# Tile halves in the output product, first rows copied by ScalarE, router sums in the retention stage

## What is computed

```python
for layer in range(DEPTH):
    y = _even_mixer(h, ...) if layer % 2 == 0 else _odd_mixer(h, ...)
    h = _layer_norm(DN_ALPHA * h + y, ln_w[layer, 0], ln_b[layer, 0])
    y = _moe(h, router_w, moe_w_gate[layer], moe_w_up[layer], moe_w_down[layer])
    h = _layer_norm(DN_ALPHA * h + y, ln_w[layer, 1], ln_b[layer, 1])

def _moe(h, router_w, w_gate, w_up, w_down):
    probs = softmax(x @ router_w)
    # the best group of four experts, and the top two inside it
    # tokens sorted by expert; hid = silu(x @ w_gate[e]) * (x @ w_up[e]); y = hid @ w_down[e]
```

## Time and profile before

| | before |
|---|---|
| median of 3 runs | 1387.13 us (1386.0 to 1387.42) |
| the profiled execution | 1386.77 us |
| its span in the trace | 1384.9 us |
| TensorE busy | 1335.2 us, 96% |
| VectorE busy | 528.3 us, 38% |
| chain of work that ended last | PE 86%, DVE 9% |
| granted TensorE clock, mean | 0.983 |

### The profile page before, as it was taken

One profiled execution on the slowest core, in us unless ns is written; L12 is line 12 of the kernel. 1 busy time (PEld: TensorE's weight loads), 2 busy tenths in 40 slices (PEclk: granted clock), 3 DMA queues, 4 the chain that ended last, 5 costly groups with the idle time before them and its releaser, 6 DMA issues.

```text
span 1384.9 us, 16143 instructions
## 1 busy us (share of the span) xinstructions
PE 1335.2 (96%) x6723; PEld 604.2 (44%) x6723; DVE 528.3 (38%) x1008; ACT 189.8 (14%) x319; POOL 167.2 (12%) x126
## 2 busy tenths in 40 slices
PE   8999999989999999999999999999898899999996
PEld 4444464533333333344555555555545333333332
DVE  1344762453111111430365666665636221111117
ACT  0025400100000000011111111111111000000000
POOL 0000400041000000200122332222300500000011
PEclk9999989999999999999999999999999999999998
DMA  9920065188999997643321122200094789999943
GB/s 352 370 74 1 31 273 212 53 318 312 410 420 406 422 405 290 247 116 111 90 61 37 25 61 61 61 0 0 4 390 182 294 327 426 402 427 407 426 178 150
DMA packets 83993, 305.84 MB, mean 221 GB/s; under 512 B 6516, under 2 KB 50904, under 8 KB 71512
## 3 DMA queue, kind: packets, MB, share of 16 engines
q1 hardware_dynamic: 61872, 264.65, 49.0%
q10 hardware_dynamic: 17448, 23.46, 4.7%
q0 software_dynamic: 4608, 16.78, 3.2%
HBM read 271.31 MB, written 33.55 MB: 220 GB/s over the span
## 4 chain that ended last, share of the span: by engine, by line
PE 86%; DVE 9%; DMA 1%; issue 1%; ACT 1%; POOL 0%; DVEq 0%; POOLq 0%; SPq 0%
PE ps L596 24%; PE ps L759 14%; PE ps L631 12%; PE ps L475 8%; PE ps L553 7%; PE ps L746 4%; PE ps L781 4%; PE ps L811 2%; PE ps L581 2%; PE ps L545 1%; DVE S L1590 1%; PE ps L534 1%; PE ps L619 1%; PE ps L799 1%; PE ps L521 1%
## 5 line engine op out<-in xcount | busy, mean ns | idle before, releaser
L596 PE MATMUL ps<-W,S 128*32 128x512 f32 (+1 forms) x2048 | 338.5, 600 | 2.2 <-DVE S L1513 2.2
L759 PE MATMUL ps<-hT,W 128*128 128x512 f32 x512 | 232.6, 593 | 0.7 <-ACT W L890 0.7
L596 PE MATMUL ps<-S 128*64 128x512 f32 (+1 forms) x512 | 224.8, 597 | 0.4 <-DVE S L1513 0.4
L631 PE MATMUL ps<-W,hT 128*32 128x512 f32 (+1 forms) x1024 | 171.5, 601 | 1.0 <-DVE hT L1527 1.0
L596 PEld LDWEIGHTS ps<-W,S 128*32 128x32 f32 (+1 forms) x2048 | 97.6, 114 | 150.1 <-issue 145.8
L759 PEld LDWEIGHTS ps<-hT,W 128*128 128x128 f32 x512 | 92.9, 191 | 90.3 <-issue 88.4
L631 PE MATMUL ps<-S,hT 128*32 128x512 f32 (+1 forms) x256 | 113.0, 594 | 1.0 <-DVE hT L1527 1.0
L890 ACT ACTIVATE hT<-ps 128x512 f32<-128x512 f32 x74 | 42.3, 598 | 376.7 <-PE ps L631 287.0
L596 PEld LDWEIGHTS ps<-S 128*64 128x64 f32 (+1 forms) x512 | 62.1, 124 | 71.8 <-issue 70.5
L1721 POOL TENSOR_TENSOR W<-S,sq 128x256 f32<-128x256 f32 x64 | 73.5, 1149 | 160.9 <-PE ps L781 117.3
L475 PE MATMUL ps<-W,hT 128*128 128x512 f32 x192 | 85.5, 604 | 2.1 <-DMA W<-w_in_even 2.1
(11 more groups left out here) (246 smaller groups left out, 1346.7 us busy)
## 6 DMA issues: line engine op xcount, KB each, us to landing
W<-moe_w_gate SPq DMA_DIRECT2D x24, 2048.0 KB, 12.3
W<-moe_w_up SPq DMA_DIRECT2D x24, 2048.0 KB, 13.1
W<-moe_w_down SPq DMA_DIRECT2D x24, 2048.0 KB, 11.4
S<-moe_w_gate SPq DMA_DIRECT2D x8, 2048.0 KB, 13.5
S<-moe_w_up SPq DMA_DIRECT2D x8, 2048.0 KB, 13.8
S<-moe_w_down SPq DMA_DIRECT2D x8, 2048.0 KB, 16.7
W<-w_in_odd SPq DMA_DIRECT2D x32, 512.0 KB, 6.3
slot_rows<-S ACTq DMA_DIRECT2D x4, 2816.0 KB, 20.0
```

The lines of the kernel that those rows point to most:

```text
L596: last = pe.matmul(ps[a:a + n, bank, :], xgT[:, c, a:a + n], w[L][slot_of(e)][:, c, :], start=(c == 0), stop=(c == ND - 1))
L631: last = pe.matmul(ps[a:a + n, 2 + half, :], hidT[:, c, a:a + n], wd[L][slot_of(e)][:, c, half * 512:(half + 1) * 512], start=(c == 0), st ...
L759: last = pe.matmul(ps[:, f % 2, :], ring[slot][:, f, c, :], hT[:, c, :], start=(c == 0), stop=(c == ND - 1))
```

## The change

It has four parts.

1. **Router sums later.** `router_sums(0)` and `router_spread(0)` leave the input projections on PE. They now stand in the retention loop (after the scores of head 1, and after the scores of head 3) in bank 7. VectorE's `router_terms(0)` follows the `prob` of head 1 and `spread_terms(0)` the `prob` of head 2, ahead of the `head_norm` of head 0.
2. **Tile 3 in halves.** Half 0 of tile 3 is transposed inside output product k = 7, in place of the second half of tile 2's logits; these follow behind the product (`last_logits`). VectorE adds and measures half 0 of tile 3 before half 1 is there, and ScalarE copies each half as it comes.
3. **Centre of tile 3 later.** `centre` of tile 3 moves from ahead of `route` to just ahead of tile 3's `shift`, between the third and the fourth selection. PE's products with the selections run tile by tile, both halves of each.
4. **ScalarE copies the first rows.** Half 1 of the first rows, and both transposed halves, are copied by ScalarE in place of VectorE. PE waits for `slots_done` before `up(0)`, since `up(0)` writes the bank that the slots are computed from.

The core of the diff (the same edits as at `logits(0, ...)` stand for layer 1, and the `halves` arguments are passed through in `turn_h`, `turn_copies`, `scale_output`, `statistics` and `add`):

```diff
-            project(4)
-            router_sums(0, 3)
-            project(5)
-            router_spread(0, 3)
-            for n in (6, 7):
+            for n in range(4, 8):
                 project(n)
...
             for hd in range(HR):
                 if hd + 1 < HR:
                     scores(hd + 1)
+                if hd == 0:
+                    router_sums(0, 7)
+                elif hd == 2:
+                    router_spread(0, 7)
                 pe.wait_ge(prob_done, (hd + 1) * NT)
...
+            def last_logits(L):
+
+                logits(L, 2, range(4, ND))
+                turn_h(2 * L + 1, NT - 1, (1,))
+                logits(L, NT - 1, range(4))
+                logits(L, NT - 1, range(4, ND))
...
-                for half in range(2):
-                    for t in range(NT):
-                        pe.wait_ge(sel_done, L * NT + t + 1)
+                for t in range(NT):
+                    pe.wait_ge(sel_done, L * NT + t + 1)
+                    for half in range(2):
                         last = pe.matmul(ps[:, 2 + half, :], first_sel[:, t, :], h[:, t, half * 512:(half + 1) * 512],
                                          start=(t == 0), stop=(t == NT - 1))
-                    last.then_inc(side_ps, 1)
+                        if t == NT - 1:
+                            last.then_inc(side_ps, 1)
...
                     gate(u)
+                    if u == 0:
+                        pe.wait_ge(slots_done, L + 1)
                     up(u)
...
                     out_project(k, mixT, w_out0, range(4), True, False)
                     logits(0, 1)
-                    logits(0, 2)
+                    turn_h(1, NT - 1, (0,))
+                    logits(0, 2, range(4))
                     out_project(k, mixT, w_out0, range(4, ND), False, True).then_inc(op_ps, 1)
...
-            turn_h(1, NT - 1)
-            logits(0, NT - 1)
+            last_logits(0)
             spin(1, 6)
...
                 copy(first_rows[:, 0:512], ps[:, 2, :]).then_inc(side_copied, 1)
+                act.wait_ge(side_ps, 3 * L + 2)
+                copy(first_rows[:, 512:1024], ps[:, 3, :]).then_inc(side_copied, 1)
+                for half in range(2):
+                    act.wait_ge(xgT_ps[L], half + 1)
+                    copy(xgT[:, half * 4:half * 4 + 4, :],
+                         ps[:, 4 + half, :].rearrange("p (c n) -> p c n", c=4)).then_inc(xgT_done[L], 1)
...
+                if hd == 1:
+                    router_terms(0)
+                elif hd == 2:
+                    spread_terms(0)
                 if hd >= 2:
                     head_norm(hd - 2)
...
-                add(3)
-                statistics(n, 3)
+                add(3, (0,))
+                v.bn_stats(col("st", 0, 6), h[:, 3, 0:512])
+                add(3, (1,))
+                statistics(n, 3, (1,))
                 for t in range(3):
                     scaled_logits(L, t)
-                centre(n, 3)
+                dve.wait_ge(std_done, n * NT + 4)
+                done(v.reciprocal(col("rst1", 3, 1), col("std", 3, 1)))
                 done(scaled_logits(L, 3))
...
                     if t == NT - 1:
+                        centre(2 * L, t)
                         shift(t)
...
-                dve.wait_ge(side_ps, 3 * L + 2)
-                v.tensor_copy(first_rows[:, 512:1024], ps[:, 3, :]).then_inc(side_copied, 1)
-                copy_rows(0)
                 hidden(0, first=True)
```

More of the change, by code:

```diff
@@ L429, in _, with turn_h @@
         def _(pe):
-            def turn_h(n, t):
+            def turn_h(n, t, halves=(0, 1)):
                 if n == 0:
@@ L434, in turn_h @@
                 elif n % 2:
-                    pe.wait_ge((op_used, op_added)[n // 2], 2 * t + 2)
+                    pe.wait_ge((op_used, op_added)[n // 2], 2 * t + halves[-1] + 1)
                 else:
                     pe.wait_ge(ln_done, (n - 1) * NT + t + 1)
-                for half in range(2):
+                for half in halves:
                     for c in range(4):
@@ L555, in out_project, with logits @@
                 return last
-            def logits(L, t):
-                pe.wait_ge(hT_done, (2 * L + 1) * 2 * NT + 2 * t + 2)
+            def logits(L, t, chunks=range(ND)):
+                pe.wait_ge(hT_done, (2 * L + 1) * 2 * NT + 2 * t + (1 if chunks[-1] < ND // 2 else 2))
                 pe.wait_ge(prmC, L + 2)
-                for c in range(ND):
+                for c in chunks:
                     last = pe.matmul(ps[:, 0 if t < NT - 1 else 2, t * NE:(t + 1) * NE], hT[:, c, t * P:(t + 1) * P], rw[:, c, :],
                                      start=(c == 0), stop=(c == ND - 1))
-                last.then_inc(logits_ps, 1)
+                if chunks[-1] == ND - 1:
+                    last.then_inc(logits_ps, 1)
+            def last_logits(L):
[3 more added lines that the diff above has]
+                logits(L, NT - 1, range(4, ND))
             def router(L):
@@ L871, in _ @@
                     logits(1, 1)
-                    logits(1, 2)
+                    turn_h(3, NT - 1, (0,))
+                    logits(1, 2, range(4))
                     out_project(k, OG, w_out1, range(4, HG), False, True).then_inc(op_ps, 1)
@@ L879, in _ @@
                     logits(1, 0)
-            turn_h(3, NT - 1)
-            logits(1, NT - 1)
+            last_logits(1)
             spin(1, 6)
@@ L890, in copy, with turn_copies @@
                 return nc.scalar.activation(o, i, ACT.Copy)
-            def turn_copies(n, t):
-                for k in (2 * t, 2 * t + 1):
+            def turn_copies(n, t, halves=(0, 1)):
+                for k in (2 * t + half for half in halves):
                     act.wait_ge(hT_ps, n * 2 * NT + k + 1)
@@ L1114, in _, with scale_output @@
             act.wait_ge(rms_done, 1)
-            def scale_output(t):
-                for k in (2 * t, 2 * t + 1):
+            def scale_output(t, halves=(0, 1)):
+                for k in (2 * t + half for half in halves):
                     act.wait_ge(op_ps, 2 * NT + k + 1)
@@ L1132, in _ @@
             turn_copies(3, 2)
-            scale_output(3)
-            turn_copies(3, 3)
+            for half in range(2):
+                scale_output(3, (half,))
+                turn_copies(3, 3, (half,))
             norm_std(2, 3)
@@ L1194, in _ @@
             v.tensor_tensor(col("lbe", 8, 8), lb1, col("lbm"), ALU.subtract).then_inc(prm_sub, 1)
-            spread_terms(0)
             for n in range(LRU_BLOCKS):
@@ L1303, in tile_of, with statistics @@
                 return halves, ps[:, 2 * t:2 * t + 2, :] if n % 2 else halves
-            def statistics(n, t):
+            def statistics(n, t, halves=(0, 1)):
                 _, src = tile_of(n, t)
-                for half in range(2):
+                for half in halves:
                     last = v.bn_stats(col("st", 6 * half, 6), src[:, half, :])
@@ L1372, in add_mixer, with add @@
             def add_mixer(L):
-                def add(t):
-                    for half in range(2):
+                def add(t, halves=(0, 1)):
+                    for half in halves:
                         k = 2 * t + half
@@ L1384, in add @@
                                                    ).then_inc(op_added, 1)
-                    dve.wait_ge((op_used, op_added)[L], 2 * t + 2)
+                    dve.wait_ge((op_used, op_added)[L], 2 * t + halves[-1] + 1)
                 return add
```

15 lines of the change are left out of this document (7 added, 8 removed).

## The result

The change takes **1379.66 us** (median of 5 runs, 1378.46 to 1380.36) against 1387.13 before: a ratio of 0.9948, 95% interval 0.9934 to 0.9963, or 7.2 us less. I had forecast 1382.9 and a range down to 1380.3.

A forecast was written before the change was run, and what follows sets the result against it. TensorE, busy 96% of the span, was taken as the bound. Terms -4.7 and -5.5 (turns), +2.8 (retention), +3.0 (clock) and +0.1 gave -4.3 us, forecast 1382.9; 8-in-10 range 1380.3 to 1386.0.

The forecast's parts named there:

- VectorE's stand: Retention, ahead of the spread terms: VectorE stands 7 us for the router spread, queued on PE behind head 3's scores.
- PE's wait: Retention, ahead of head 3's pv: PE stands +2.8 us for `prob`, bounds 0 and 4.
- Gate(0) at 20.8 us behind k = 7: Layer 0, sign to look for: the first expert product starts about 20.8 us behind k = 7's end, 25.9 before.
- the clock's term: Low clock behind three new PE gaps, in retention and ahead of each layer's `turn_rows(1)`: 1.0 us each, +3.0.
- Layer 0's turn: Layer 0, `turn_rows(1)`: PE waits 2.5 us for sorted rows and turns them at 307.7, not 312.41: -4.7 us.
- Layer 1's turn: Layer 1, `turn_rows(1)`: sorted rows bound the turn, at 1091.8 against 1097.34: -5.5 us.
- For PE the centre is hidden: Selections: PE works through the first three meanwhile, covering the centre's 1.27 us; without that cover, up to 1.3 cost.
- that case: First rows copied by VectorE behind the slots: gate(0) 1.0 us earlier per layer, gain 2 in all ahead of retention's cost.
- rival 4: First rows: ScalarE's copies come late and PE's arrival bounds the turn; same time as forecast, chance contained in it.
- Rival 1: Low stretches follow all three gaps, spin costs 1: at most 1387.7 us, about 1385.8 with half; chance 0.24.
- Rival 2: Retention: the low clock stays for its whole rest behind the gap ahead of head 3's pv: 1392.7 us; chance 0.06.
- Rival 3: Retention: spread ready before VectorE arrives, so 2.8 and its 1.0 of clock drop out: 1379.1 us; chance 0.06.

The follow-up runs named there:

- the second profile of the change: The changed kernel once more, unedited, on another chip: 1380.78 us, ratio 0.9948 to the kernel before.
- the two experiments: Centre of tile 3 put back ahead of `route`: in the change 1384.20 us, in the change with the spread one head earlier 1380.34 us.
- experiment 6: The change with VectorE again copying half 1 of the first rows and both transposed halves: 1385.58 us, ratio 0.9988 to the kernel before.
- experiments 4: The kernel before with only the router sums and spread moved into retention: 1390.24 us, ratio 1.0016 to the kernel before.
- experiment 7: The change with tile 3 whole instead of in halves, in both layers: 1384.93 us, ratio 0.9982 to the kernel before.
- experiment 8: The change with the spread one head earlier, plus more unread spin products around the count of tokens: 1378.18 us, ratio 0.9931 to the kernel before.

## Why the prediction was wrong in size and right in direction

**The single waits held, the sum did not.** VectorE's stand was forecast at 7 us and is 7.04; PE's wait at 2.8 and is 2.61. `route` begins 3.8 us behind the start of the last add (3.7 forecast). In layer 1 PE waits for the rows and turns them 4.4 us sooner behind k = 7 (5.05 forecast). Gate(0) at 20.8 us behind k = 7 came only with more spin (21.6); in the change it is 24.5 and 23.8. Without the clock's term the forecast's sum is -7.3 us, that is 1379.8, where 1379.7 was measured. That is luck: the two turns gave 1.8 less than their terms, and in the two profiles side by side 3.45 of the 7.6 us lie in the fourth and the last stretch of the table, whose terms are 0.45 and 0.

**The step that failed is the clock's: "Three new gaps ... I take 1.0 each, +3.0".** The term counted only stretches that the new gaps might add, and took the low stretches that were there already to stay or to be worth nothing. It failed in its sign for the kernel as a whole: the mean granted clock rose from 0.983 to 0.987 over the runs. Were all of that time on the path, it would be 5.5 us (an estimate from the two clocks), where I had only let it fall; how much of the 5.5 is on the path stays open. The three gaps themselves cost some 1.4 us of low clock, nearly all of it in retention, and not 3.0:

- *Retention*: a low stretch of 3.4 us followed in five of six profiles, 1.4 us on average. 1.0 was right in size, even a little low, and the 3.8 for part 1 as a whole agree with 1.8, 2.2 and 4.7 by the runs and 4.0 by the profiles.
- *Layer 0's turn*: the gap isn't there, one of the things by which I said I would be wrong. The rows landed where they were forecast, 37.4 us behind k = 7 (37.2), but PE came 1.0 later. I had not seen the wait of 2.05 us ahead of the count, behind which the selections run low: 10.10 us in place of 6.9. That used up the slack ahead of the rows. It is why this layer gives 3.1 and not 4.25.
- *Layer 1's turn*: PE waited 1.7 us and the clock stayed. In the second profile of the change it didn't wait at all and came 1.1 us behind the rows, with gaps in up(0). Behind the 2.9 us wait of the run with the sums back the clock did fall (at 1088.2), so the fear was not empty, but the change's gap is shorter.

**What the sum lacked is part 2's second effect.** I priced tile 3's halves by what they shorten, 1.0 in each layer. Taken out they cost 4.7 us, put in they give 4.2, each with about 3 either way. One piece of that was seen: up to 1.7 us that k = 7 lost to the low clock in layer 0, in four of the five profiles with tile 3 whole and in two of the eight with halves. With 2.0 less for the two turns, 2.7 more for part 2 and the 1.8 that the turns fell short, the forecast's -4.3 becomes -7.2. That this meets the measured value is no proof: single terms are uncertain by more than 1 us.

**"For PE the centre is hidden"** holds as far as the selections go. That the sorted rows bound the turn holds for layer 1 in the first profile of the change; in layer 0, and for layer 1 in the second, PE comes 0.9 to 1.1 us behind them. The centre's move is worth 3.2 and 4.4 us by the two experiments, more than its 1.27 in each layer. That it also keeps PE's idle time ahead of the count short (2.05 against 3.15 us) fits that, but wasn't tested by itself.

**The copies.** 0.60 us on ScalarE against 0.67 on VectorE held again. The Trainium skill (ScalarE: Activation LUTs, Rules for kernel authors) says to use VectorE for the elementwise operations that it lists, `add` and `mul` among them; a copy out of PSUM is not in that list. With VectorE's copies the change is worth 1.7 us (experiment 6), against the 2 less retention's cost that I gave that case, and with ScalarE 7.2. The measurement decides for ScalarE where VectorE has a table of slots ahead of it. Its table load of 1.28 us came behind the copies, at 298.77, so rival 4's late copies didn't arise. Its other half did, by the selections' low clock: in layer 0 PE's arrival bounds the turn.

**The rivals.** Rival 1 (the clock takes it back) fell: no gap at a turn was followed by a low stretch in the change. Its page, the Trainium skill (TensorE: Matmul & The Clock Gate, HAM oscillation), tells of waits for DMA of about 3 to 5 us, each followed by the half rate. The waits here are shorter: behind 2.6 us in retention the trace agrees in five of six profiles, behind 1.7 us in layer 1 it doesn't. Rival 2 fell: the low stretch in retention was a single one in every profile. Rival 3 didn't occur in the change, but is what moving the spread a head earlier makes: 4.7 us less, with 3.5 either way, where I had given it 3.8.

**What stays open:** how much of the miss the clock explains, since tile 3 whole has the change's mean clock and is 4.7 us slower; why the mean clock rises with part 3 beside part 4 (0.986 to 0.987, against 0.984 for part 4 alone or the change without it) and the time hardly follows it; the gaps in up(0) under full DMA; and the middle stretch's scatter of 4 us.

## What to carry to other kernels

When an edit takes work off a saturated engine, list what that engine did just before its next wait, and whether it ran low there: a low stretch on work that only fills a wait costs nothing, and when it goes, the next work may get it. So price both signs of the clock, for the stretches that are there as for the gaps that are new, and take several profiles for it. Put a small product that another engine waits for ahead of the long group, not behind it: here 0.40 us of work one head earlier took away a wait of 2.6 us and the low stretch behind it, some 4 us in all. A higher granted clock is a gain only where nothing slower (here the DRAM trip of the sorted rows) ends the wait.

## What the runs showed of the hardware that I had not expected

- From the end of the selections to gate(0) PE does nothing but eight transposes. Where that took 4.9 to 5.7 us (before, experiments 4 and 6) a low stretch lay on gate(0) five times of five; with ScalarE's copies it takes 2.6 us, and none did in the 20 cases of ten profiles. A wait of 2.6 us without a break in retention: five of six. One of 2.04 to 3.16 us ahead of the count: 15 of 15, on the selections.
- A low stretch can also begin in the middle of work, behind 3.64 us of 128x16 products in which PE counts as busy all the time (experiment 7: the next product of 3.68 us took 5.38). It did so in six of ten layers with 32 such products in a row and in four of sixteen with the row broken up, so it isn't shown that the row is the cause.
- At full clock and without a recorded wait, PE's rate in up(0) fell from 24 to 18 and 9 recorded products in 2.00 us while the DMA share was 0.99 and 0.96; at a share of 0.92, just before, it was still 24 (experiment 8). Seen on two chips of three.
- The low stretches lie elsewhere in each execution, and the runs of one kernel spread over 2 to 10 us (before: 1381.7 to 1391.3 on one chip). A single profile can't tell a part's worth of 2 us; it can show what a wait is made of.
